# A streaming-encoder layer on one core: the first modulation's LayerNorm moves to ScalarE, and TensorE's and ScalarE's small steps between a quarter's units change order

## The chip, the cores and the metric

The kernel runs on one core of one Trainium2 chip. The metric is the device time of one execution in microseconds (us), and the number compared is the median over runs.

## The reference

One layer over 256 tokens (two blocks of 128 partitions) of width D = 2048, all in float32. What matters here is its very start:

```
ada = silu(c) @ w_ada + b_ada                  # c is one row of 2048, w_ada is 2048 x 12288
shift1, scale1, gate1, shift2, scale2, gate2 = split(ada, 6)
h = layer_norm(x) * (1 + scale1) + shift1      # x is 256 x 2048; no gain and no bias in this norm
q_a, kv_a, ... = split(h @ w_in)               # the first two slabs of 512 columns feed the attention branch
```

layer_norm subtracts the mean over the 2048 columns and multiplies by 1/sqrt(variance + 1e-5). Behind it come latent attention, a state-space branch, the merge of the two, an output projection, and an expert layer that gathers 128 rows per token from two tables. None of that is touched.

## The kernel before

Every engine runs its own hand-written list of instructions, and only semaphores tie the lists together. The first stage works in four **quarters** q = 0 to 3, each for 512 of the 2048 columns of x.

**The modulation of a quarter.** The columns of w_ada for the quarter's shift and scale (1024 columns) come in eight chunks of 1 MiB, 32 in all, numbered here c0 to c31 (c8q to c8q+7 belong to quarter q). SP issues their transfers (L585) into five buffers in turn, so chunk n waits until chunk n-5 has been used. Two 1 MiB loads of projection weights (`raw`, L572) stand behind the first chunk of quarters 1, 2 and 3, and the last two behind c31. VectorE uses the first seven chunks of a quarter (`ada1_chunks`, L1645 and L1647, two instructions a chunk, 128x1024 each), and sums into `ada1_acc`. TensorE uses the eighth, its own chunk, in `ada1_rest(q)` (L757, 32 matmuls of one column), and then adds up VectorE's partial sums over the partitions in `ada1_sums(q)` (L766, 16 matmuls of one column). `mod_quarter(q)` on VectorE (L1661, L1663) adds the bias `b_ada` and writes shift and scale to `adacol`.

**x.** Two transfers (L592) are issued behind c4. VectorE takes mean and variance (`normalise`: L1600, L1605), ScalarE the root (L1156), VectorE the reciprocal (L1595) and the normalised x in place (L1612), once for each block of tokens. TensorE transposes x in four groups (L780), ScalarE copies each out of PSUM into `xnT` (L1197).

**A quarter of h.** ScalarE applies scale and shift to the four 128-row tiles of the quarter (L1204) and rounds them to `h_hi` (L1208). VectorE takes the remainder `h_lo` (`h_quarter`, L1670). Each quarter then has two projection **units** (s = 0 and 1, one for each slab): ScalarE rounds the unit's weights to `whi` (`hi`, L1141), VectorE takes the remainder `wlo` (`lo`, L1578), and TensorE does 16 matmuls of 512 columns on `whi` (L691, L692) and 8 on `wlo` (L697) in `token_unit`. A unit starts on `h_ready` and `hi_ready`, and its last 8 matmuls wait for `lo_ready`.

**Order on each engine, as written.** VectorE: c0 to c6; the copies of `cols` and `keysT` out of PSUM (L1676, L1678), which wait for the small parameters; LayerNorm of x; then for q = 1 to 3: three chunks of quarter q, mod_quarter(q-1), one chunk, h_quarter(q-1), a chunk, lo, a chunk, lo, a chunk; at the end mod_quarter(3), h_quarter(3) and two lo. TensorE: transposes of the parameters (L741, L744, behind all 17 small loads, `params_in`); ada1_rest(0), ada1_sums(0); the transposes of x; then for each quarter both units, and behind them ada1_rest(q+1) and ada1_sums(q+1). ScalarE: SiLU of c, exp of `A_log` (which waits for `params_in`), the two roots of x, four copies of transposed x, then for each quarter scale and shift, `h_hi`, and the two `hi`.

The next stage begins with ScalarE's sums of squares of the two slabs (L1217) and a root (L1156), VectorE's `rms`, and two narrower units (L716, L717, L722).

Of the kernel before, what the change touches and what calls it, by code (L numbers as in the profile page):

```python
# [13 lines left out]
ALU = mybir.AluOpType  # L14
# [4 lines left out]
P = 128  # L19
D = 2048  # L20
# [50 lines left out]
U_LOW = 0  # L71
# [63 lines left out]
def build(nc, a, out, stop="all"):  # L135
    ctx = ExitStack()
    with ctx:
# [14 lines left out]
        def sem(name):  # L152
            return ctx.enter_context(nc.semaphore(name))
# [39 lines left out]
        x_in = at("x_in", 126 * KB, [P, BLK, D])  # L193
        xnT = at("xnT", 142 * KB, [P, DC, SEQ])
# [328 lines left out]
        ln2_step = sem("ln2_step")  # L523
        x1_ready = sem("x1_ready")
        var_ready = sem("var_ready")
        std_ready = sem("std_ready")
# [141 lines left out]
        def _(pe):  # L668
# [70 lines left out]
            pe.wait_ge(params_in, 16 * 17)  # L739
            for j, (first, n) in enumerate(((0, COLS_T1), (COLS_T1, P), (COLS_T2, COLS_ALL - COLS_T2))):  # L740
                last = nc.tensor.transpose(aux[:, 0, first:first + n], rows[0:n, j, :], ident[0:n, 0:n])  # L741
            last.then_inc(rows_turned, 1)
            for j in range(2):
                last = nc.tensor.transpose(aux[:, 1, j * P:j * P + P], krows[:, j, :], ident)  # L744
            last.then_inc(rows_turned, 1)
# [26 lines left out]
            ada1_sums(0)  # L772
            pe.wait_ge(x_normed, BLK)
            pe.wait_ge(cols_ready, 2)
# [15 lines left out]
            if on("low"):  # L790
# [10 lines left out]
                for q in range(QUARTERS):  # L801
                    pe.wait_ge(h_ready, q + 1)
                    for s in range(2):
                        token_unit(U_LOW, 2 * q + s, 0, 0, h_hi, h_lo, 4 * q, DC - 1,
                                   [ps[:, s, b, :] for b in range(BLK)], early=True)
                    if q + 1 < QUARTERS:
                        ada1_rest(q + 1)
                        ada1_sums(q + 1)
# [324 lines left out]
        def _(act):  # L1133
# [55 lines left out]
            F(csil[:, :], aux[:, 2, 0:DC], ACT.Silu).then_inc(c_ready, 1)  # L1189
            act.wait_ge(params_in, 16 * 17)  # L1190
            F(anegA[:, :], anegA[:, :], ACT.Exp).then_inc(neg_a, 1)
            for b in range(BLK):
                norm_root(b + 1)
# [6 lines left out]
            for q in range(QUARTERS):  # L1200
                act.wait_ge(h_full, q + 1)
# [7 lines left out]
                for s in range(2):  # L1209
                    hi(U_LOW, 2 * q + s, 0, 0)  # L1210
# [207 lines left out]
            if on("h2"):  # L1418
                for b in range(BLK):
                    norm_root(b + 3, b)  # L1420
                for b in range(BLK):
# [3 lines left out]
                    act.wait_ge(ln2_step, 3 * b + 1)  # L1425
                    F(minus_mean, total, ACT.Copy, scale=-1.0 / D).then_inc(ln2_step, 1)
                    act.wait_ge(ln2_step, 3 * b + 2)
                    F(ln2_junk[:, :], x1[:, b, :], ACT.Square, bias=minus_mean, accum_out=square).then_inc(ln2_step, 1)
                    act.wait_ge(ln2_step, 3 * b + 3)
# [139 lines left out]
        def _(dve):  # L1569
# [103 lines left out]
            dve.wait_ge(c_ready, 1)  # L1673
            ada1_chunks(0, 0, ADA_V)
            dve.wait_ge(rows_turned, 1)
            V.tensor_copy(cols[:, :], aux[:, 0, 0:COLS_ALL]).then_inc(cols_ready, 1)  # L1676
            dve.wait_ge(rows_turned, 2)
            V.tensor_copy(keysT[:, :, :].rearrange("p a b -> p (a b)"), aux[:, 1, 0:2 * KEYS]).then_inc(cols_ready, 1)  # L1678
            dve.wait_ge(x_loaded, 16 * BLK)
            for b in range(BLK):  # L1680
                normalise(x_in[:, b, :], x_in[:, b, :], b + 1).then_inc(x_normed, 1)
            for q in range(1, QUARTERS):
                ada1_chunks(q, 0, 3)
                mod_quarter(q - 1)
                ada1_chunks(q, 3, 4)
                h_quarter(q - 1)
                for s in range(2):
                    ada1_chunks(q, 4 + s, 5 + s)
                    lo(U_LOW, 2 * (q - 1) + s, 0, 0)
                ada1_chunks(q, 6, ADA_V)  # L1690
# [563 lines left out]
        def _(pool):  # L2254
# [87 lines left out]
            if on("all"):  # L2342
# [22 lines left out]
                for r in range(BLK * SEL):  # L2365
# [6 lines left out]
                    elif r < EARLY:  # L2372

                        pool.wait_ge(x1_stored, 16 * BLK)
                        pool.wait_ge(ln2_step, 3 * BLK)
# [74 lines left out]
```

## Time and profile before

| | us |
|---|---|
| three runs: median | 2737.41 |
| lowest and highest | 2735.43 and 2744.17 |
| span of the profiled execution, first to last instruction | 2736.6 |
| TensorE busy in it | 2371.4 (87%) |
| VectorE busy in it | 2055.5 (75%) |
| ScalarE busy in it | 1007.8 (37%) |
| GpSimd busy in it | 883.5 (32%) |

The profiled execution has no time of its own beside the span, so the span is what it is held to: it is 0.8 us under the median of the three runs. The stage that is changed is the first of many; it ends at about 148 us of the span, when the eighth projection unit is done. The rest of the span is the same code in both kernels.

### The profile page before, as it was taken

The page shows a single profiled execution, that of the slowest core. Times are in us where ns is not written, and L with a number is a line of the kernel's source. Part 1 is how long each engine was busy: PE and PEld are TensorE (multiplying, and loading weights), DVE is VectorE, ACT ScalarE, POOL GpSimd, SP SyncE. Part 2 cuts the span into 40 slices and gives each one's busy share as a digit, 9 for nine tenths or more (in the row PEclk, how much of TensorE's full clock was granted, in tenths as well). Part 3 has the DMA queues.
Part 4 walks back from the last instruction along what each step waited for, and adds up shares of the span by engine and source line. Part 5 has one row for each costly group of instructions (what it writes and reads, how often), then busy time and mean ns, then how long its engine had stood idle before and what let it go on. Part 6 is the DMA issues. An engine that isn't in the chain of part 4 may idle for free.

```text
span 2736.6 us, 38178 instructions
## 1 busy us (share of the span) xinstructions
PE 2371.4 (87%) x14404; PEld 1975.2 (72%) x14404; DVE 2055.5 (75%) x2511; ACT 1007.8 (37%) x1436; POOL 883.5 (32%) x745
## 2 busy tenths in 40 slices
PE   3799999999999999999969776666667699999994
PEld 3689999888888889999859766656566664444441
DVE  6777679778888786444575899999999786665577
ACT  2245443344444444433343222227777750000000
POOL 0000011222222220000001466656666554444354
PEclk9799999999999999999989888887777799999997
DMA  9766669566666665555745999999999879999997
GB/s 381 290 216 239 218 236 345 209 216 216 216 215 216 213 212 177 185 185 184 264 181 191 355 410 419 420 403 392 405 407 399 348 259 414 413 414 414 414 412 254
DMA packets 143723, 817.88 MB, mean 299 GB/s; under 512 B 16552, under 2 KB 19232, under 8 KB 69328
## 3 DMA queue, kind: packets, MB, share of 16 engines
q0 software_dynamic: 93200, 477.21, 44.7%
q1 hardware_dynamic: 48480, 335.95, 33.2%
q10 hardware_dynamic: 1888, 2.59, 0.3%
q8 instruction: 106, 1.74, 0.3%
q14 instruction: 49, 0.40, 0.0%
HBM read 811.46 MB, written 4.23 MB: 298 GB/s over the span
## 4 chain that ended last, share of the span: by engine, by line
PE 63%; DVE 25%; issue 4%; DMA 4%; ACT 3%; POOL 1%; ACTq 0%; DVEq 0%; POOLq 0%
PE aux L1122 15%; DVE rrow L2145 12%; PE ps L716 9%; PE ps L717 9%; PE ps L722 9%; PE ps L691 4%; PE ps L692 4%; PE ps L697 3%; DVE rrow_first L2145 2%; DVE ada_acc L1647 1%; PE aux L973 1%; DMA dskip<-in_D_skip 1%; DMA ada_in<-in_p_ada 1%; DMA vden<-in_p_vd 1%; PE aux L930 1%
## 5 line engine op out<-in xcount | busy, mean ns | idle before, releaser
L1578 DVE TENSOR_TENSOR wlo<-raw,whi 128x2048 fp32r<-128x2048 f32 x216 | 497.3, 2303 | 323.0 <-ACT whi L1141 312.8
L1141 ACT ACTIVATE whi<-raw 128x2048 fp32r<-128x2048 f32 x216 | 412.2, 1911 | 685.3 <-PE ps L722 528.0
L2175 DVE SCALAR_TENSOR_TENSOR ps<-vrow,acc,ps 128x1024 f32<-128x1024 f32 x235 | 302.6, 1288 | 176.4 <-DMA vrow<-in_p_vg,acc 156.7
L2354 POOL DMA_INDIRECT rrow<-in_peer_u,acc x222 | 359.8, 1621 | 220.1 <-DVE dots L2145 115.3
L2145 DVE CUSTOM_DVE_ANT_0 rrow<-rrow,h 128x2048 f32<-128x2048 f32 x175 | 391.1, 2289 | 9.1 <-DMA rrow<-in_peer_u,acc 8.6
L716 PE MATMUL ps<-h_hi,whi 128*128 128x256 f32 x1552 | 389.2, 291 | 1.3 <-DVE h_lo L2033 1.3
L717 PE MATMUL ps<-h_lo,whi 128*128 128x256 f32 x1552 | 377.0, 283 | 0.0
L2354 POOL DMA_INDIRECT vrow<-in_p_vg,acc x256 | 252.3, 986 | 255.5 <-DVE ps L2175 173.5
L716 PEld LDWEIGHTS ps<-h_hi,whi 128*128 128x128 f32 x1552 | 297.9, 192 | 16.2 <-issue 14.1
L717 PEld LDWEIGHTS ps<-h_lo,whi 128*128 128x128 f32 x1552 | 298.2, 192 | 5.8 <-issue 5.7
L1064 PE MATMUL aux<-hT,rT 128*128 128x128 f32 x1792 | 235.8, 295 | 72.6 <-ACT rT L1472 71.8
L1064 PEld LDWEIGHTS aux<-hT,rT 128*128 128x128 f32 x1792 | 228.1, 210 | 82.6 <-issue 68.4
L2268 POOL DMA_DIRECT2D ada_in<-in_p_ada x128 | 69.3, 542 | 675.6 <-DVEq L1734 534.3
L1122 PE MATMUL aux<-vden,wt 128*128 128x512 f32 x512 | 241.5, 594 | 0.0
L1627 DVE SCALAR_TENSOR_TENSOR acc<-ada_in,csil,acc 128x512 f32<-128x512 f32 x240 | 184.8, 770 | 37.0 <-DMA ada_in<-in_p_ada 24.2
L722 PE MATMUL ps<-h_hi,wlo 128*128 128x256 f32 x1552 | 202.1, 283 | 0.0
L722 PEld LDWEIGHTS ps<-h_hi,wlo 128*128 128x128 f32 x1552 | 193.3, 192 | 0.0
L1156 ACT ACTIVATE st<-st,con 128x2 f32<-128x2 f32 (+1 forms) x18 | 5.2, 294 | 507.4 <-DVE st L1605 507.1
L1122 PEld LDWEIGHTS aux<-vden,wt 128*128 128x128 f32 x512 | 97.8, 191 | 123.6 <-issue 123.6
L1472 ACT ACTIVATE rT<-ps 128x1024 f32<-128x1024 f32 x112 | 110.8, 1021 | 173.1 <-PE ps L1054 165.7
L1086 PE MATMUL aux<-oh 128*128 128x128 f32 x512 | 87.8, 333 | 93.8 <-ACT oh L1518 87.7
L1054 PE MATMUL ps<-con,rrow 128*128 128x128 f32 x752 | 128.5, 344 | 40.9 <-DMA rrow<-in_peer_u,acc 40.9
(353 smaller groups left out, 4318.9 us busy)
## 6 DMA issues: line engine op xcount, KB each, us to landing
raw<-in_p_in SPq DMA_DIRECT2D x104, 1024.0 KB, 4.9
ada_in<-in_p_ada POOLq DMA_DIRECT2D x128, 512.0 KB
vden<-in_p_vd SPq DMA_DIRECT2D x64, 1024.0 KB
ada_in<-in_p_ada SPq DMA_DIRECT2D x32, 1024.0 KB, 9.2
raw<-in_p_so SPq DMA_DIRECT2D x32, 1024.0 KB, 4.8
raw<-in_p_mo SPq DMA_DIRECT2D x16, 1024.0 KB, 7.1
raw<-in_p_bc SPq DMA_DIRECT2D x16, 1024.0 KB, 7.1
raw<-in_p_mix SPq DMA_DIRECT2D x16, 1024.0 KB, 4.8
```

The lines of the kernel that those rows point to most:

```text
L716: mm(o, wh, x_hi[:, k, :], start=(k == 0 and first), stop=False, skip_group_check=True)
L717: mm(o, wh, x_lo[:, k, :], start=False, stop=False, skip_group_check=True)
L722: last = mm(o, lo[:, kc, c:c + width], x_hi[:, k, :], start=False, stop=(k == klast), skip_group_check=True)
L1054: last = nc.tensor.transpose(ps[:, half, t // 4, (t % 4) * P:(t % 4) * P + P], row_tile(r)[:, c:c + P], ident)
L1064: last = mm(aux[:, 3, j * P:j * P + P], rT[:, kc, :], hT[b][:, kc, :], start=(kc == 0), stop=(kc == DC - 1), skip_group_check=True)
L1122: last = mm(aux[:, 2 * b + n, :], wt_column(b, 2 * u + q), vden[:, u % 4, q, n * W:n * W + W], start=(u == 0 and q == 0), stop=(u == NVU - ...
L1141: F(whi[:, n % 2, :, 0:cols_], raw[:, n % 4, :, 0:cols_], ACT.Copy).then_inc(hi_ready, 1)
L1578: V.tensor_tensor(wlo[:, n % 2, :, 0:cols_], raw[:, n % 4, :, 0:cols_], whi[:, n % 2, :, 0:cols_].bitcast(F32), ALU.subtract).then_inc(lo_ ...
L1627: last = V.scalar_tensor_tensor(acc_, tile[:, kc, :], csil[:, k:k + 1], acc_, ALU.mult, ALU.add)
L2145: last = V.tensor_tensor_reduce(row, row, h2[:, b, :], 1.0, 0.0, ALU.mult, ALU.add, dots[:, k, e:e + 1])
L2175: last = V.scalar_tensor_tensor(o, row, w, o, ALU.mult, ALU.add)
L2354: return G.indirect_dma_start(out=dst, out_offset=None, in_=table, in_offset=bass.IndirectOffsetOnAxis(ap=eid_all[:, r:r + 1], axis=0))
```

## The change

There are four edits.

1. The statistics of x move from VectorE to ScalarE: for each block a Copy that sums, the negated mean, a Square around the mean that sums, and the root (three steps on `x_step`, with the scratch tile `x_junk` at the place of `xnT`). VectorE only takes the reciprocal and the product of the negated mean with it (`mean_and_root`), and ScalarE then writes the normalised x with one Identity per block. exp of `A_log` moves behind it. Since `x_step` and the later second norm share a semaphore, the later waits are raised by 6.
2. TensorE's transposes of the parameters move from ahead of ada1_rest(0) to behind ada1_sums(0), and VectorE's copies of their results from ahead of quarter 1 into it, behind its first two chunks. mod_quarter(q-1) comes behind two chunks of quarter q instead of three, and everything behind it follows one chunk earlier.
3. ada1_rest(q+1) goes between a quarter's two units, and ada1_sums(q+1) behind the second.
4. ScalarE rounds the first weights of a quarter (`hi` of unit 2q) ahead of the wait for that quarter's shift and scale, not behind `h_hi`.

```diff
--- before.py
+++ after.py
@@ -191,6 +191,7 @@
         h2 = at("h2", 110 * KB, [P, BLK, D])
 
         x_in = at("x_in", 126 * KB, [P, BLK, D])
+        x_junk = at("x_junk", 142 * KB, [P, D])
         xnT = at("xnT", 142 * KB, [P, DC, SEQ])
         oT = at("oT", 126 * KB, [P, DC, SEQ])
         cqT_hi = at("cqT_hi", 142 * KB, [P, RC, SEQ], F32R)
@@ -521,8 +522,10 @@
         row_used = sem("row_used")
         scale_plus = sem("scale_plus")
         ln2_step = sem("ln2_step")
+        x_step, x_steps = ln2_step, 3 * BLK
         x1_ready = sem("x1_ready")
         var_ready = sem("var_ready")
+        x_scaled = var_ready
         std_ready = sem("std_ready")
         fin_ready = sem("fin_ready")
         out_done = sem("out_done")
@@ -736,13 +739,6 @@
             pe.wait_ge(con_in, 16)
             pe.wait_ge(c_in, 16)
             nc.tensor.transpose(aux[:, 2, 0:DC], crow[:, :], ident[0:DC, 0:DC]).then_inc(c_turned, 1)
-            pe.wait_ge(params_in, 16 * 17)
-            for j, (first, n) in enumerate(((0, COLS_T1), (COLS_T1, P), (COLS_T2, COLS_ALL - COLS_T2))):
-                last = nc.tensor.transpose(aux[:, 0, first:first + n], rows[0:n, j, :], ident[0:n, 0:n])
-            last.then_inc(rows_turned, 1)
-            for j in range(2):
-                last = nc.tensor.transpose(aux[:, 1, j * P:j * P + P], krows[:, j, :], ident)
-            last.then_inc(rows_turned, 1)
 
             ada_sum = aux[:, 3, :]
 
@@ -770,8 +766,14 @@
             pe.wait_ge(c_ready, 1)
             ada1_rest(0)
             ada1_sums(0)
+            pe.wait_ge(params_in, 16 * 17)
+            for j, (first, n) in enumerate(((0, COLS_T1), (COLS_T1, P), (COLS_T2, COLS_ALL - COLS_T2))):
+                last = nc.tensor.transpose(aux[:, 0, first:first + n], rows[0:n, j, :], ident[0:n, 0:n])
+            last.then_inc(rows_turned, 1)
+            for j in range(2):
+                last = nc.tensor.transpose(aux[:, 1, j * P:j * P + P], krows[:, j, :], ident)
+            last.then_inc(rows_turned, 1)
             pe.wait_ge(x_normed, BLK)
-            pe.wait_ge(cols_ready, 2)
             for r in range(4):
                 if r >= 2:
                     pe.wait_ge(xT_ready, r - 1)
@@ -803,9 +805,8 @@
                     for s in range(2):
                         token_unit(U_LOW, 2 * q + s, 0, 0, h_hi, h_lo, 4 * q, DC - 1,
                                    [ps[:, s, b, :] for b in range(BLK)], early=True)
-                    if q + 1 < QUARTERS:
-                        ada1_rest(q + 1)
-                        ada1_sums(q + 1)
+                        if q + 1 < QUARTERS:
+                            (ada1_sums if s else ada1_rest)(q + 1)
 
                 for k in range(2):
                     channel_unit(U_LOW, 8 + k, 0, 0, h_hi, h_lo, DC // 2 * k, DC - 1,
@@ -1187,10 +1188,25 @@
 
             act.wait_ge(c_turned, 1)
             F(csil[:, :], aux[:, 2, 0:DC], ACT.Silu).then_inc(c_ready, 1)
+            act.wait_ge(con_in, 16)
+            act.wait_ge(x_loaded, 16 * BLK)
+            for b in range(BLK):
+                total, minus_mean, square = (st[:, 52 + 3 * b + j:53 + 3 * b + j] for j in range(3))
+                if b:
+                    act.wait_ge(x_step, 3 * b)
+                F(x_junk[:, :], x_in[:, b, :], ACT.Copy, accum_out=total).then_inc(x_step, 1)
+                act.wait_ge(x_step, 3 * b + 1)
+                F(minus_mean, total, ACT.Copy, scale=-1.0 / D).then_inc(x_step, 1)
+                act.wait_ge(x_step, 3 * b + 2)
+                F(x_junk[:, :], x_in[:, b, :], ACT.Square, bias=minus_mean, accum_out=square).then_inc(x_step, 1)
+                act.wait_ge(x_step, 3 * b + 3)
+                root(st[:, 46 + 4 * b:47 + 4 * b], square, 1.0 / D)
+            for b in range(BLK):
+                act.wait_ge(x_scaled, b + 1)
+                F(x_in[:, b, :], x_in[:, b, :], ACT.Identity, scale=st[:, 46 + 4 * b:47 + 4 * b],
+                  bias=st[:, 44 + 4 * b:45 + 4 * b]).then_inc(x_normed, 1)
             act.wait_ge(params_in, 16 * 17)
             F(anegA[:, :], anegA[:, :], ACT.Exp).then_inc(neg_a, 1)
-            for b in range(BLK):
-                norm_root(b + 1)
 
             for r in range(4):
                 act.wait_ge(x_turned, r + 1)
@@ -1198,6 +1214,7 @@
                   psf[:, 1024 * (r % 2):1024 * (r % 2) + 1024], ACT.Copy).then_inc(xT_ready, 1)
 
             for q in range(QUARTERS):
+                hi(U_LOW, 2 * q, 0, 0)
                 act.wait_ge(h_full, q + 1)
                 act.wait_ge(xT_ready, 4 + q)
                 for k in range(4 * q, 4 * q + 4):
@@ -1206,8 +1223,7 @@
                 last.then_inc(xT_ready, 1)
                 act.wait_ge(xT_ready, 4 + q + 1)
                 F(h_hi[:, 4 * q:4 * q + 4, :], xnT[:, 4 * q:4 * q + 4, :], ACT.Copy).then_inc(h_hi_ready, 1)
-                for s in range(2):
-                    hi(U_LOW, 2 * q + s, 0, 0)
+                hi(U_LOW, 2 * q + 1, 0, 0)
             if on("low"):
                 def sumsq(s):
                     for b in range(BLK):
@@ -1422,11 +1438,11 @@
                     act.wait_ge(x1_ready, b + 1)
                     total, minus_mean, square = (st[:, 52 + 3 * b + j:53 + 3 * b + j] for j in range(3))
                     F(ln2_junk[:, :], x1[:, b, :], ACT.Copy, accum_out=total).then_inc(ln2_step, 1)
-                    act.wait_ge(ln2_step, 3 * b + 1)
+                    act.wait_ge(ln2_step, x_steps + 3 * b + 1)
                     F(minus_mean, total, ACT.Copy, scale=-1.0 / D).then_inc(ln2_step, 1)
-                    act.wait_ge(ln2_step, 3 * b + 2)
+                    act.wait_ge(ln2_step, x_steps + 3 * b + 2)
                     F(ln2_junk[:, :], x1[:, b, :], ACT.Square, bias=minus_mean, accum_out=square).then_inc(ln2_step, 1)
-                    act.wait_ge(ln2_step, 3 * b + 3)
+                    act.wait_ge(ln2_step, x_steps + 3 * b + 3)
                     root(st[:, 46 + 4 * b:47 + 4 * b], square, 1.0 / D)
                 for b in range(BLK):
                     for q in range(4):
@@ -1671,23 +1687,31 @@
                                 h_hi[:, 4 * q:4 * q + 4, :].bitcast(F32), ALU.subtract).then_inc(h_ready, 1)
 
             dve.wait_ge(c_ready, 1)
+            def mean_and_root(b):
+
+                rsqrt(st[:, 46 + 4 * b:47 + 4 * b], b + 1)
+                V.tensor_tensor(st[:, 44 + 4 * b:45 + 4 * b], st[:, 53 + 3 * b:54 + 3 * b], st[:, 46 + 4 * b:47 + 4 * b],
+                                ALU.mult).then_inc(x_scaled, 1)
+
             ada1_chunks(0, 0, ADA_V)
-            dve.wait_ge(rows_turned, 1)
-            V.tensor_copy(cols[:, :], aux[:, 0, 0:COLS_ALL]).then_inc(cols_ready, 1)
-            dve.wait_ge(rows_turned, 2)
-            V.tensor_copy(keysT[:, :, :].rearrange("p a b -> p (a b)"), aux[:, 1, 0:2 * KEYS]).then_inc(cols_ready, 1)
-            dve.wait_ge(x_loaded, 16 * BLK)
             for b in range(BLK):
-                normalise(x_in[:, b, :], x_in[:, b, :], b + 1).then_inc(x_normed, 1)
+                mean_and_root(b)
             for q in range(1, QUARTERS):
-                ada1_chunks(q, 0, 3)
+                ada1_chunks(q, 0, 2)
+                if q == 1:
+                    dve.wait_ge(rows_turned, 1)
+                    V.tensor_copy(cols[:, :], aux[:, 0, 0:COLS_ALL]).then_inc(cols_ready, 1)
+                    dve.wait_ge(rows_turned, 2)
+                    V.tensor_copy(keysT[:, :, :].rearrange("p a b -> p (a b)"), aux[:, 1, 0:2 * KEYS])\
+                        .then_inc(cols_ready, 1)
+                    dve.wait_ge(cols_ready, 1)
                 mod_quarter(q - 1)
-                ada1_chunks(q, 3, 4)
+                ada1_chunks(q, 2, 3)
                 h_quarter(q - 1)
                 for s in range(2):
-                    ada1_chunks(q, 4 + s, 5 + s)
+                    ada1_chunks(q, 3 + s, 4 + s)
                     lo(U_LOW, 2 * (q - 1) + s, 0, 0)
-                ada1_chunks(q, 6, ADA_V)
+                ada1_chunks(q, 5, ADA_V)
             mod_quarter(QUARTERS - 1)
             h_quarter(QUARTERS - 1)
             for s in range(2):
@@ -2372,7 +2396,7 @@
                     elif r < EARLY:
 
                         pool.wait_ge(x1_stored, 16 * BLK)
-                        pool.wait_ge(ln2_step, 3 * BLK)
+                        pool.wait_ge(ln2_step, x_steps + 3 * BLK)
                         pool.wait_ge(x1_ready, BLK)
                     elif r < EARLY + 4:
```

## Rows read from the trace of the kernel before

**Rows 1.** Timeline, 0 to 59 us: start, duration, engine, line, form, count, idle before it.

```profile
26.03 5.33 DVE L1647 SCALAR_TENSOR_TENSOR ada_acc<-ada_in,csil,ada_acc 128x1024 f32<-128x1024 f32 x4 [2.07 <-DMA ada_in<-in_p_ada]
...
35.20 0.86 PE L741 MATMUL aux<-con,rows 120*128 120x120 f32 x3 [30.70 <-DMA dskip<-in_D_skip]
...
36.29 6.83 PE L757 MATMUL aux<-csil,ada_in 128*128 128x1 f32 x32
...
46.05 0.74 DVE L1645 TENSOR_SCALAR ada_acc<-ada_in,csil 128x1024 f32<-128x1024 f32 x1
...
46.39 5.86 PE L780 MATMUL ps<-con,x_in 128*128 128x128 f32 x32
...
50.08 3.23 ACT L1197 ACTIVATE xnT<-ps 128x1024 f32<-128x1024 f32 x3 [0.68 <-PE ps L780]
```

**Rows 2.** Timeline, the modulation of quarter 0 and the start of quarter 1's.

```profile
53.43 0.16 DVE L1661 TENSOR_TENSOR adacol<-aux,cols 128x4 f32<-128x4 f32 x1
...
53.83 2.07 ACT L1204 ACTIVATE xnT<-xnT,adacol 128x256 f32<-128x256 f32 x4 [0.52 <-DVE adacol L1663]
...
56.90 3.70 ACT L1141 ACTIVATE whi<-raw 128x2048 fp32r<-128x2048 f32 x2
57.09 1.23 DVE L1670 TENSOR_TENSOR h_lo<-xnT,h_hi 128x1024 fp32r<-128x1024 f32 x1 [0.79 <-ACT h_hi L1208]
...
58.93 0.77 PE L691 MATMUL ps<-whi,h_hi 128*128 128x512 f32 x1 [6.68 <-ACT whi L1141]
...
78.12 0.16 DVE L1661 TENSOR_TENSOR adacol<-aux,cols 128x4 f32<-128x4 f32 x1
```

**Rows 3.** Timeline, VectorE: a chunk that was late, and quarter 3's modulation.

```profile
99.71 5.25 DVE L1647 SCALAR_TENSOR_TENSOR ada_acc<-ada_in,csil,ada_acc 128x1024 f32<-128x1024 f32 x4 [2.21 <-DMA ada_in<-in_p_ada]
...
129.26 0.16 DVE L1661 TENSOR_TENSOR adacol<-aux,cols 128x4 f32<-128x4 f32 x1 [7.18 <-PE aux L766]
```

**Rows 4.** Stretches: from:to, us, busy by engine, PEclk, DMA share, GB/s.

```profile
58.93:77.80 18.87, 18.82 (x96) 16.18 (x96) 18.30 (x14) 1.66 (x1) 0.00 (x0) 0.86 0.85 321
110.49:129.25 18.76, 18.73 (x96) 16.15 (x96) 11.41 (x8) 1.66 (x1) 0.00 (x0) 0.86 0.53 213
58.93:67.06 8.13, 8.13 (x25) 6.51 (x26) 7.99 (x6) 1.66 (x1) 0.00 (x0) 0.68 1.01 419
118.50:123.93 5.43, 5.43 (x27) 4.49 (x26) 3.54 (x3) 0.00 (x0) 0.00 (x0) 1.00 0.36 124
123.93:129.25 5.32, 5.29 (x47) 5.21 (x47) 0.00 (x0) 0.00 (x0) 0.00 (x0) 0.98 0.00 0
129.25:134.76 5.51, 0.00 (x1) 0.04 (x1) 1.66 (x4) 5.08 (x7) 0.00 (x0) 0.50 0.00 0
158.40:166.00 7.60, 7.60 (x51) 7.60 (x52) 7.22 (x23) 1.86 (x3) 0.00 (x0) 0.78 0.75 277
```

**Rows 5.** Tile ln_junk: the same two steps in the later norm, durations in ns min/median/max.

```profile
L1424 ACT ACTIVATE ln_junk<-x x2: 1909/1909/1909, 1410.2 to 1415.0; 128x2048 f32<-128x2048 f32 x2
...
L1428 ACT ACTIVATE ln_junk<-x,st x2: 2002/2002/2002, 1412.5 to 1417.3; 128x2048 f32<-128x2048 f32 x2
```

**Rows 6.** Stretches of ten us: transfers at full load, and with a pause.

```profile
20.00:30.00 10.00, 0.00 (x0) 0.00 (x0) 7.67 (x6) 0.00 (x0) 0.00 (x0) 1.00 1.00 395
...
70.00:80.00 10.00, 7.75 (x60) 7.24 (x58) 9.50 (x11) 1.49 (x3) 0.00 (x0) 0.89 0.72 257
```

**Rows 7.** Timeline, SP: the issue of c20, c21 and c22.

```profile
76.00 1.29 SPq L585 DMA_DIRECT2D ada_in<-in_p_ada  x3
```

**Rows 8.** Timeline, TensorE behind the changed stage: two short stops.

```profile
156.41 0.41 PE L817 MATMUL aux<-con,dk 128*128 128x128 f32 x2 [0.90 <-ACT dk L1242]
158.37 0.39 PE L716 MATMUL ps<-cqT_hi,whi 128*128 128x256 f32 x1 [1.55 <-DVE wlo L1578]
```

**Rows 9.** Timeline, ScalarE: a table load behind the changed stage, and what follows it.

```profile
150.75 1.28 ACT L1238 ACT_TABLE_LOAD   x1
152.05 0.40 ACT L1238 ACTIVATE sin<-angs 128x64 f32<-128x64 f32 x2
```

## The prediction

> **What bounds the kernel now.** I read first the timeline of the first 60 us, then that of VectorE and TensorE to the end of the changed stage, then stretches for the clock and the transfers. About 0.8 us lies between the profiled span and the median, so differences of the span are taken over as they are. What measurement can tell from no change is 0.3%, about 8.2 us.
>
> The start [rows 1]: c5 arrives at 26.0, VectorE is done with c6 at 31.4 and then waits for TensorE's transposes of the parameters, which start at 35.20 when the last small load is in. Copies and LayerNorm of x follow, and quarter 1's first chunk is used only at 46.05. TensorE meanwhile works through its own chunk and the sums (36.29 to 46.39, 10.1 us), transposes x in 5.86 us, and ScalarE ends its last copy at 53.3. The modulation of quarter 0 is at 53.43 [rows 2], so there VectorE's list and the path of x end together. That is the place to look at twice: freeing one of the two gives only the distance to the other.
>
> From then on one pattern repeats [rows 2]. From mod_quarter to the end of h_lo are 4.89 us (53.43 to 58.32), and TensorE starts the quarter at 58.93, 5.50 us behind mod_quarter, because the first `whi` (half of a pair of 3.70 us from 56.90) is ready at 58.8, half a us behind h_lo. From the end of h_lo to the next mod_quarter are 19.80 us (58.32 to 78.12) of VectorE without a pause: six chunks of at most 2.65 [rows 1] and two `lo`. TensorE's share of a quarter, two units, its own chunk and the sums, is 18.87 and 18.76 us [rows 4]. VectorE leads in the first two quarters. In quarter 2 it also waited 2.21 us for c25, which came in at 99.6; quarter 3's modulation at 129.26 waited 7.18 us for TensorE's sums [rows 3]. So the last quarter is TensorE's, and it starts at 129.26 + 5.50 = 134.76. Everything later hangs on that start.
>
> **The change part by part.**
>
> *Statistics on ScalarE.* The two passes are known from the later norm, 1.91 and 2.00 us [rows 5]. x stands just ahead of c5 in the queue, one MiB takes 2.65 us at 395 GB/s [rows 6], so x is in by 23.4. With 1 us a block allowed for the small steps and one table load of 1.28 [rows 9], ScalarE has the second root at 23.4 + 2 x 4.9 + 1.3 = 34.5; VectorE adds 0.4, and the two Identity passes, priced as the Copy of 1.91, end at 38.9. Moving exp of `A_log` behind them costs nothing: its result is used much later.
>
> *TensorE's start.* Its own chunk c7 is in two transfers behind c5, at 31.3 [rows 1, 6]. Own chunk and sums 10.1, up to 41.4; transposes of the parameters 1.1 (35.20 to 36.29), up to 42.5. The normalised x has been there since 38.9 (cover 3.6 us; if ScalarE needs more than that, every us counts). Transposes 5.86, up to 48.4, last copy 1.1, 49.5. ScalarE now does `hi` of unit 0 ahead of the scaling, 1.9, so that scaling starts at 51.4 in place of 53.83. mod_quarter(0) isn't late: VectorE uses c8 and c9, copies the parameters, and passes it near 45. Then it uses c10 (to 48) and stands still for some 7 us until h_hi. This is where the 14.7 us that VectorE saves (31.4 to 46.05) go: all but 2.4 become waiting. h_lo ends at 58.32 - 2.4 = 55.9, and with `whi` ready the quarter's units start 0.13 behind it, at 56.05 in place of 58.93.
>
> *The chunk order.* Behind h_lo come four chunks instead of three, and ahead of the next mod_quarter two instead of three: again six chunks and two `lo`, 19.80. VectorE would pass mod_quarter(1) at 75.7.
>
> *Weights ahead.* TensorE starts 4.89 + 0.13 = 5.0 behind mod_quarter in place of 5.50: 0.5 us, which count where the quarter's path runs through it. `hi` has its data: the last pair of loads stands behind c31, and from 110.49 to 129.25 the transfers were busy for only 0.53 of the time [rows 4], so they were done before 121. Were one late, the scaling behind it on ScalarE would be late by as much.
>
> *Transfers.* c12 waits for TensorE's use of c7, now done near 38 instead of 43. c20 waited for TensorE's use of c15 and was issued at 76.00 [rows 7], and the transfer engines idled 0.28 of the ten us around it, 2.8 us [rows 6]. With c15 used between the units (56.05 + 8.13 + 3.5 = 67.7) that wait goes. Against it, c16 is issued when c11 is used, and that is now behind h_lo (58.5 instead of 56.3), 2.1 later. I take the difference: c25 comes at 98.9, within bounds of 96.8 and 99.6. VectorE wants it at 97.8, so mod_quarter(2) is no earlier than 98.9 + 2.6 = 101.5.
>
> *Own chunk between the units.* In sum TensorE's 18.8 us stay the same. Its sums are then done at 56.05 + 18.87 = 74.9, ahead of VectorE. But 32 matmuls of one column, 3.5 us (two thirds of the 5.32 us that they and the 16 of the sums take), now stand between two units of 512 columns. In the rows [rows 4] the granted clock was at the higher level (2.4 GHz) in a second unit (1.00, 5.43 us), and after 5.3 us of one-column work it had fallen to the lower (1.2 GHz): 0.98 up to 129.25, 0.50 in the pause behind. A shorter slack shows too: behind the stage TensorE stopped 0.9 us, did two small transposes, and stopped 1.55 us more [rows 8], and in the stretch that followed the clock was 0.78, so 0.44 of 7.6 us at the lower level, 3.3 us, of which half, 1.7, is lost [rows 4]. The new gap lies between the two in length. Call the loss in a quarter p: below 0, as no such dip; the row nearest in length gives 1.7, which I take for each of three quarters; at the most every matmul of the own chunk and of the second unit runs at half rate, 3.5 + 5.4 = 8.9.
>
> The Trainium skill (TensorE: Matmul & The Clock Gate, HAM oscillation) says that a pause between bursts of matmuls throttles the clock again, so that each burst starts at the lower rate; it speaks against this edit. By it each second unit starts slow, as a first one does (8.13 against 5.43), so p would be 2.7 and the sum below put the last start at 135.6 instead of 132.6; that the clock falls behind long one-column work, the rows agree.
>
> *A table load.* exp now stands behind the roots, so the root for the first slab must load its table again, 1.28 us [rows 9]. It falls while unit 7 runs (5.4 us), most of it covered; bounds 0 and 1.3, taken 0.3. The Trainium skill (ScalarE: Activation LUTs, What ACT_TABLE_LOAD costs) puts 2.66 us on a switch, a drain with it; the row shows the next activation 1.30 behind the load's start, and the row decides.
>
> **The sum, p = 1.7.** Sums of quarter 1: 56.05 + 18.87 + 1.7 = 76.6 (VectorE 75.7), start of its units 81.6. Sums of quarter 2: 81.6 + 18.8 + 1.7 = 102.1 (c25 allows 101.5), start 107.1. Sums of quarter 3: 107.1 + 18.8 + 1.7 = 127.6, against 129.26. Start of the last units 132.6, against 134.76: 2.2 us. With the table load 1.9, so 2737.4 - 1.9 = 2735.5.
>
> **The rivals.**
>
> *No dip* (p = 0). Modulations at 75.7, 101.5 (c25 leads), 101.5 + 5.0 + 18.8 = 125.3, last start 130.3: 4.5 earlier, 2733.2 with the table load. For it: the gap is shorter than the 5.3 us behind which the fall shows. Against: the dip behind the two short stops.
>
> *A full second warm-up*, p of 2.4 to 3. The last start is 127.5 + 3p, so at 2.4 the gain is gone; at 3, 136.5: 1.7 later, 2739.4. No change that can be measured.
>
> *Slower.* One mechanism: the clock goes down during each own chunk and stays down through the second unit. With p = 8.9 the last start is 127.5 + 26.7 = 154.2, 19.4 later: 2757. It becomes measurable from p = 5.1 on. Against: a first unit after a pause of 5.5 us got through in 8.13 at a mean of 0.68, so the clock came back within it.
>
> *VectorE's saving goes through.* If the path of x is shorter than worked out (TensorE at full rate at the start), VectorE leads, and the floor is the transfers: what they idled, some 4 us up to c25 and about as much behind it, gives at most 8 us: 2729.4. Against: TensorE's one-column matmuls took 6.83 us there.
>
> *It doesn't act.* If x is normalised later than 46.4, the start doesn't move, and with the dips the time is 2738 to 2740.
>
> **How the numbers follow.** Forecast with dips 0.42, no dip 0.28, full warm-up 0.14, no action 0.05, VectorE's saving 0.07, slower 0.04. The first four are all within 0.3% (0.89). Faster by more takes the far end of the fifth and errors of several terms: 0.07. Slower: 0.04. The range takes in all but the fifth's end and the slower case: 2730 to 2741; the forecast's own is 2733 to 2738, by c25's bounds, the table's and p of 1 to 2.4.
>
> **What the profile would show.** Units of quarter 0 start near 56, behind a stand of VectorE of some 7 us between c10 and h_lo; ScalarE's roots near 34.5; own chunk of quarter 1 at 64 to 68, c20 issued near 71; a clock below 1.00 in the second units; modulation of quarter 3 near 127.6; a new table load at L1156 near 140. Wrong would make it above all a start far from 56 (the rate of the first one-column matmuls), and p.

## The result, and the profile after

The changed kernel takes 2745.26 us (median of 9 executions, 2742.28 to 2749.39) against 2736.54 for the kernel before (9, 2733.95 to 2744.17). The ratio is 1.0029, with a 95% interval of 1.0021 to 1.0038: a slowdown of 0.3%, some 8 us, where 1.9 us of gain were forecast. The profiled execution took 2742.28 us, its fastest, and its span is 2740.6, so 1.7 us lie between the two.

The stage that was changed did what was forecast of it. Timeline of the changed kernel, 20 to 56 us, all engines:

```profile
31.40 6.96 PE L753 MATMUL aux<-csil,ada_in 128*128 128x1 f32 x32 [27.09 <-DMA ada_in<-in_p_ada]
...
33.36 0.29 ACT L1157 ACTIVATE st<-st,con 128x1 f32<-128x1 f32 x1
33.56 4.06 ACT L1206 ACTIVATE x_in<-x_in,st 128x2048 f32<-128x2048 f32 x2
...
38.22 3.55 PE L762 MATMUL aux<-con,ada_acc 128*128 128x1 f32 x16
...
42.69 4.17 PE L782 MATMUL ps<-con,x_in 128*128 128x128 f32 x24
...
50.95 2.06 ACT L1221 ACTIVATE xnT<-xnT,adacol 128x256 f32<-128x256 f32 x4
...
54.20 1.23 DVE L1686 TENSOR_TENSOR h_lo<-xnT,h_hi 128x1024 fp32r<-128x1024 f32 x1 [6.64 <-ACT h_hi L1225]
...
55.48 0.79 PE L694 MATMUL ps<-whi,h_hi 128*128 128x512 f32 x1 [7.29 <-DVE h_lo L1686]
```

Read it against [rows 1, 2]. TensorE's first work moves from 35.20 to 31.40, the second root is at 33.36, the normalised x is there at 37.6 (33.56 + 4.06) and waits for TensorE, and VectorE stands still for 6.64 us ahead of `h_lo`: what it saved became waiting. The quarter's units start at 55.48 instead of 58.93. The steps of VectorE and the last quarter's first unit, timelines of the same kernel:

```profile
75.66 0.16 DVE L1677 TENSOR_TENSOR adacol<-aux,cols 128x4 f32<-128x4 f32 x1
...
98.27 2.60 DVE L1663 SCALAR_TENSOR_TENSOR ada_acc<-ada_in,csil,ada_acc 128x1024 f32<-128x1024 f32 x2 [0.59 <-DMA ada_in<-in_p_ada]
...
101.55 0.16 DVE L1677 TENSOR_TENSOR adacol<-aux,cols 128x4 f32<-128x4 f32 x1 [0.68 <-PE aux L762]
...
126.39 0.16 DVE L1677 TENSOR_TENSOR adacol<-aux,cols 128x4 f32<-128x4 f32 x1 [5.11 <-PE aux L762]
...
131.26 0.79 PE L694 MATMUL ps<-whi,h_hi 128*128 128x512 f32 x1 [4.91 <-DVE h_lo L1686]
```

From quarter 2 on each modulation waits for TensorE's sums (101.55 and 126.39), and the last units start 3.5 us earlier than before (131.26 against 134.76 in the prediction's sum). Stretches of the changed kernel show what the new place of the own chunk costs (columns as in [rows 4]): an own chunk between the units, the three second units, and quarter 2's whole share.

```profile
62.78:66.53 3.75, 3.75 (x33) 3.75 (x32) 3.68 (x4) 1.34 (x1) 0.00 (x0) 0.93 1.01 428
66.53:73.42 6.89, 6.89 (x25) 5.59 (x26) 6.10 (x6) 0.57 (x1) 0.00 (x0) 0.79 0.98 369
...
92.40:99.61 7.21, 7.21 (x27) 5.72 (x27) 6.26 (x7) 1.91 (x1) 0.00 (x0) 0.76 1.02 425
...
117.56:124.51 6.95, 6.95 (x25) 5.64 (x26) 3.65 (x3) 0.00 (x0) 0.00 (x0) 0.78 0.23 85
...
106.49:126.35 19.86, 19.86 (x96) 17.06 (x96) 14.54 (x10) 2.33 (x2) 0.00 (x0) 0.82 0.63 257
```

The second unit of each quarter ran at a mean granted clock of 0.76 to 0.79 instead of 1.00. With the own chunk ahead of it, it took 10.6 us (3.75 + 6.89; then 3.49 + 7.21 and 3.67 + 6.95) instead of 8.9 (3.5 of the 5.32 us of one-column work in [rows 4], and 5.43): 1.7, 1.8 and 1.7 us.

A quarter's whole share grew by other amounts: 19.78, 20.85 and 19.86 us, against 18.87, 18.78 and 18.76 in the kernel before, so 0.9, 2.1 and 1.1. The first units make most of the difference: they took 7.30, 8.31 and 7.40 us, where the kernel before has 8.13, 7.78 and 8.01.

**Where the loss comes in.** ScalarE's sums of squares of the second slab close the stage. Timeline of ScalarE, the changed kernel:

```profile
139.82 1.28 ACT L1157 ACT_TABLE_LOAD   x1
...
143.84 0.60 ACT L1233 ACTIVATE junk<-ps 128x512 f32<-128x512 f32 x1 [1.47 <-PE ps L700]
```

and the same sum of squares in the kernel before:

```profile
148.05 0.60 ACT L1217 ACTIVATE junk<-ps 128x512 f32<-128x512 f32 x1 [2.75 <-PE ps L697]
```

That is 4.2 us ahead. The new table load isn't free on the way: it holds up the root and the weights behind it, and TensorE waits for `wlo`, which it did not in the kernel before. Timeline of TensorE, the changed kernel:

```profile
144.31 0.39 PE L719 MATMUL ps<-h_hi,whi 128*128 128x256 f32 x1 [0.52 <-DVE wlo L1601]
```

By 156 us TensorE is 4.2 us ahead again, so this wait is made good. Matching instructions further down, the changed kernel stays ahead, by 5.1 us at 771. Then comes VectorE's loop of the state-space stage (`with dve.Fori(1, 4)`, L1959 before and L1983 after), whose three rounds have the same code in both. VectorE across its two jumps back, the changed kernel:

```profile
771.08 1.01 DVE L1977 TENSOR_SCALAR yg<-yg,st 128x512 f32<-128x512 f32 x2
779.04 0.49 DVE L1641 TENSOR_SCALAR acc<-ada_in,csil 128x512 f32<-128x512 f32 x1 [6.95 <-issue]
...
915.21 1.01 DVE L1977 TENSOR_SCALAR yg<-yg,st 128x512 f32<-128x512 f32 x2
922.86 0.49 DVE L1641 TENSOR_SCALAR acc<-ada_in,csil 128x512 f32<-128x512 f32 x1 [6.64 <-issue]
```

and the kernel before:

```profile
776.22 1.01 DVE L1953 TENSOR_SCALAR yg<-yg,st 128x512 f32<-128x512 f32 x2
777.39 0.49 DVE L1625 TENSOR_SCALAR acc<-ada_in,csil 128x512 f32<-128x512 f32 x1 [0.16 <-issue]
...
913.41 1.01 DVE L1953 TENSOR_SCALAR yg<-yg,st 128x512 f32<-128x512 f32 x2
914.56 0.48 DVE L1625 TENSOR_SCALAR acc<-ada_in,csil 128x512 f32<-128x512 f32 x1
```

The shift (after minus before) goes from -5.1 to +1.7 over the first jump and from +1.8 to +8.3 over the second, and stays near +7 on TensorE until 1570. "issue" in the brackets means that VectorE waited for nothing that the profile shows. The queue of the instructions shows it. The transfers of the changed kernel in 774 to 781 us (queue, kind: packets, MB, share), the row of q14, the queue that reads VectorE's instructions (e3 below shows whose it is):

```profile
q14 instruction: 3, 0.02, 1.2%
```

Three reads of 8 KiB, at 774.7, 777.2 and 779.6, about 2.4 us apart; two lie in the stop, and the third begins 0.5 us after it. Between 745 and 1060 us there are ten in the changed kernel, five behind each jump, and none in the kernel before. The page of the changed kernel, its span and section 3, has

```profile
span 2740.6 us, 38182 instructions
...
q14 instruction: 59, 0.48, 0.0%
```

where the page before has

```profile
q14 instruction: 49, 0.40, 0.0%
```

So the loop's code was read again behind each jump. The loop itself is unchanged; what is new is that VectorE's list is 9 instructions shorter ahead of it (3902 in the trace against 3911, since most of LayerNorm is gone), so that the loop stands elsewhere relative to the 8 KiB pieces in which the list is read. I take a piece to hold 128 instructions, 64 bytes each; e3 bears that out.

The Trainium skill (Runtime: NRT & Kernel Launch, Instruction fetch mechanics) says that an engine has a small instruction memory, refilled in sequence by a DMA queue of its own, and that a taken jump to a target outside what it holds forces a read before execution goes on. The trace agrees with the forced read. The page's block is 16 KiB, the reads of q14 here are of 8 KiB, and the measurement decides; the other instruction queue on the page of the profile, q8, did read 16 KiB at a time (106 reads, 1.74 MB).

### The profile page after: what moved, and what is told of

Read it like the earlier page. It is cut to its first block, busy times and chain, and to the rows that moved or that the text cites. A ratio compares the mean times of both kernels' runs of the same rounds, so it can differ in the third digit from the quotient of the medians.

```text
span 2740.6 us, 38182 instructions
## 1 busy us (share of the span) xinstructions
PE 2377.4 (87%) x14404; PEld 1973.7 (72%) x14404; DVE 2050.0 (75%) x2501; ACT 1021.8 (37%) x1449; POOL 884.6 (32%) x745
## 3 DMA queue, kind: packets, MB, share of 16 engines
q8 instruction: 106, 1.74, 0.2%
## 4 chain that ended last, share of the span: by engine, by line
PE 49%; DVE 23%; DMA 14%; issue 6%; ACT 5%; POOL 2%; ACTq 0%; DVEq 0%; POOLq 0%
DMA vrow<-in_p_vg,acc 12%; DVE rrow L2169 10%; PE ps L719 9%; PE ps L720 9%; PE ps L725 9%; PE ps L694 4%; PE ps L695 4%; PE ps L700 4%; DVE rrow_first L2169 2%; DVE ps L2199 2%; POOL vrow L2378 1%; PE aux L974 1%; DMA rrow<-in_peer_u,acc 1%; PE aux L1087 1%; PE aux L931 1%
## 5 line engine op out<-in xcount | busy, mean ns | idle before, releaser
L2199 DVE SCALAR_TENSOR_TENSOR ps<-vrow,acc,ps 128x1024 f32<-128x1024 f32 x235 | 302.7, 1288 | 175.5 <-DMA vrow<-in_p_vg,acc 145.7
```

Of the source, the lines that this page charges most:

```text
L2199: last = V.scalar_tensor_tensor(o, row, w, o, ALU.mult, ALU.add)
```

## The experiments

The theory: the first stage gains about 4 us, and the place of VectorE's loop costs the rest. The rivals: the loss comes from the first stage's dips, or from the later stages' transfers being met at other times. All kernels but e2 and e8 are built on the changed kernel.

**e1: the nine instructions back.** Nine increments are added ahead of the loop by splitting two that were there (`ROWS` is 8).

```diff
-            dve.sem_inc(ada2_used, 4)
+            for n in (2, 1, 1):
+                dve.sem_inc(ada2_used, n)
...
-            dve.sem_inc(row_used, ROWS)
+            for _ in range(ROWS):
+                dve.sem_inc(row_used, 1)
```

> The changed kernel with VectorE's list made nine instructions longer at its head (two semaphore increments split into several of smaller size, while VectorE waits for the first data), so that its loop in the state-space stage stands as far into the list as in the kernel before. Theory (instruction fetch): in the changed kernel VectorE stopped 6.95 us and some 6 us at the two jumps back of that loop, with three reads of 8 KiB each on the instruction queue, because the loop stands nine instructions further forward. Then the stops and the reads are gone, the last units of the first stage still start near 131.3, and the time is that of before less some 4 us: 2732, ratio 0.9985. Rival (the later stages suffer from the shift in time itself, or from scatter): the stops stay, 2742 to 2749.

Measured: 2731.88 us (11 executions) against 2736.18, ratio 0.9991 (0.9979 to 1.0002). Nothing else differs from the changed kernel, and it is 13 us faster by the medians, some 10 by the two ratios. Against the kernel before, the interval takes in 1, so a gain of the four edits is likely but not clear of noise. Waits of VectorE, first in the changed kernel, then in e1 (what waited <- for what: us in total, times, longest):

```profile
DVE acc L1641 <- issue: 13.8, 3, 6.9
```

```profile
DVE acc L1643 <- issue: 0.2, 1, 0.2
```

and e1's page again has

```profile
span 2728.6 us, 38191 instructions
...
q14 instruction: 49, 0.40, 0.0%
```

The two stops are gone and with them the 13 us, while the first stage, dips included, is within 0.9 us of the changed kernel's (modulations at 76.01, 102.19 and 127.22, last units at 132.09). That the dips cause the loss is out.

**e2, e3: the same shift by other means.** If only the place counts, 119 instructions more (128 less 9) must put the kernel before into the same state, and 128 more must leave the changed kernel in it. The additions are waits that are already fulfilled, which take half an instruction each here: 238 ahead of the loop in the kernel before (e2), 256 in the changed kernel (e3).

```diff
             dve.sem_inc(row_used, ROWS)
+            for _ in range(238):
+                dve.wait_ge(lo_ready, 4)
```

> The kernel before with 119 more instructions at the head of VectorE's list (waits that are already fulfilled, two to an instruction), no other edit. 119 is 128 less 9, so if the list is fetched in pieces of 128 instructions (8 KiB), the loop stands in its pieces as in the changed kernel. Theory (instruction fetch): two stops of 6 to 7 us at the jumps back of the state-space loop, which the kernel before doesn't have: about 2736.5 + 13 = 2749, or somewhat less where slack takes some. Rival (scatter or the edits themselves): 2736 to 2739, no stops.

> The changed kernel with 128 more instructions at the head of VectorE's list (fulfilled waits). Control for e1: the list is longer, but by one whole piece of 128. Theory (instruction fetch, pieces of 128): the stops stay and the time is that of the changed kernel, 2745. Rival (any lengthening helps): 2732.

Measured: e2 2750.21 us (4 executions), ratio 1.0057 (1.0041 to 1.0072); e3 2747.09 (4), 1.0041 (1.0026 to 1.0057). VectorE's wait at the loop's head in e2, then in e3:

```profile
DVE acc L1627 <- issue: 14.1, 3, 7.0
```

```profile
DVE acc L1643 <- issue: 14.2, 3, 7.1
```

e2 has none of the four edits. Against the kernel before, its shift is -0.2 us at 725, +6.5 at 846 and +13.4 at 966: two stops of 6.9 and 7.0 that TensorE takes on whole. A kernel without the change thus shows the slowdown, and the changed kernel keeps it at a distance of one whole piece. In e3 the whole execution has 60 reads of q14, one more than the changed kernel's 59: 128 instructions more in VectorE's list alone are one read of 8 KiB more, so q14 is VectorE's, and 64 bytes an instruction fit. e2 has 60 too, against 49 in the kernel before: ten at the loop and one for its 119.

The added waits have a price of their own at the head: VectorE uses its first chunk at 13.50 us in e2 (11.32 before) and at 14.38 in e3 (11.22 in the changed kernel). In e2 nothing of it is left at the last units (134.22). In e3 they start at 134.79, 3.5 later than in the changed kernel, and that can make the 2 us by which e3 is slower.

**e9, e7: between.** 80 and 180 such waits in the changed kernel, 40 and 90 instructions, so 31 and 81 behind the place of the kernel before.

> The changed kernel with 40 more instructions at the head of VectorE's list, to see whether e1 works because of the number nine (the place of before) or because of a whole range of places. Theory (pieces of 128; the loop's 325 instructions touch three pieces only if it begins within the first 50 or so of one): it begins some 31 to 40 into a piece, no read on the instruction queue between the loop's first round and its end, no stops, 2732 as e1. Rival (only the place of before is free of stops): stops as in e7, 2741 or more.

> The changed kernel with 90 more instructions at the head of VectorE's list. Theory (instruction fetch, pieces of 128, and a place for few pieces; the loop has 325 instructions by the trace, so it touches three pieces only if it begins within the first 50 or so of one): the loop begins some 81 to 90 into a piece, touches four, and the two stops are there, 2745. Rival (any lengthening between 9 and 128 removes them): no stops, 2732.

Measured: e9 2732.63 us (8), ratio 0.9987 (0.9973 to 1.0001), no stop and no read of q14 between 745 and 1060 us. e7 2741.62 (8), ratio 1.0022 (1.0012 to 1.0032): slower, as the theory had it, but by less than the changed kernel and than the 2745 expected. VectorE at e7's first jump:

```profile
773.64 1.01 DVE L1979 TENSOR_SCALAR yg<-yg,st 128x512 f32<-128x512 f32 x2
779.22 0.49 DVE L1643 TENSOR_SCALAR acc<-ada_in,csil 128x512 f32<-128x512 f32 x1 [4.57 <-issue]
```

Five reads behind each jump again, but the stop is one read of 2.4 us shorter (reads at 777.2 and 779.6, so one lies in it and not two). Its whole wait there is 8.9 us against 13.8. So there are three states of the same loop: no read (places 0 and +31), stops of 4.6 and 4.3 (+81), stops of 7 (-9, which is +119). Both expectations came true in kind by some luck. They counted the 325 instructions that the trace has of a round, which would touch three or four pieces, and the reads are of five. So the loop is longer than what the trace has of it, or some reads run ahead of need.

**e4: the own chunk back behind both units.** e1 with edit 3 undone.

```diff
-                        if q + 1 < QUARTERS:
-                            (ada1_sums if s else ada1_rest)(q + 1)
+                    if q + 1 < QUARTERS:
+                        ada1_rest(q + 1)
+                        ada1_sums(q + 1)
```

> e1 with the third edit undone: TensorE's own chunk and the sums stand behind both units of a quarter again. By the terms of the prediction (p, the dip of the granted clock behind the gap): no dip in the second units, modulation of quarter 1 at 75.7 by VectorE, of quarter 2 near 100.9 by the transfers, of quarter 3 near 124.6, last units start near 129.5 in place of 131.26, so 1.8 us faster than e1. Rival (the own chunk between the units is worth something, since its buffer is free earlier): the transfers come later, and the last units start at 131 or later.

Measured: 2729.38 us (11), ratio 0.9976 (0.9967 to 0.9985), 2.5 under e1 by the medians. The profile is of its slowest execution (2736.93), and contradicts the simple picture that this place is free. Its stretches, quarter 1's share, then own chunk and sums in it alone:

```profile
80.95:102.90 21.95, 21.86 (x96) 19.11 (x96) 19.15 (x14) 2.34 (x2) 0.00 (x0) 0.73 1.01 413
...
94.66:102.82 8.16, 8.16 (x49) 8.07 (x47) 5.69 (x5) 1.06 (x1) 0.00 (x0) 0.64 1.01 410
```

Here the clock fell within the own chunk itself, in two of three quarters, the one-column work took 8.16 us and then 7.96 instead of the 5.32 of [rows 4], and the last units started at 134.61 after all. In the kernel before the clock fell only within the sums (1.93, 2.20 and 1.97 us instead of 1.84).

The profiles of all runs together say what each place costs. With the own chunk behind both units (the kernel before, e2, e4, e5, e6) TensorE's share of a quarter is 18.7 to 18.9 us in twelve of fifteen, and 21.8 to 22.0 in the three where the clock fell within the own chunk (two in e4, one in e6). With it between them (the changed kernel, e1, e3, e7, e8, e9) all eighteen take 19.8 to 21.2. The second unit is 6.89 to 7.21 us in fourteen of these, and 8.25 to 8.35 in four (one each in e1, e7, e8 and e9), each behind an own chunk of 3.9 to 4.0 us instead of 3.5. So the old place is cheaper in most quarters and dearer in some; the median puts it ahead, and the intervals of e1 and e4 meet.

**e8: edit 3 alone in the kernel before.**

> The kernel before with the third edit alone: TensorE's own chunk between a quarter's two units, the sums behind the second. VectorE's list keeps its length, so no stops at the state-space loop. Terms of the prediction: c25 comes earlier, so VectorE's wait of 2.2 us for it goes or shrinks, which brings mod_quarter(2) to about 103; a dip of the granted clock in each second unit costs 1.7 us, so quarter 3's modulation is near 128.8 to 129.5 in place of 129.26: 2736 to 2737, no change. Rival (no dip): 127.1, 2734.5. Rival (full second warm-up, 3 us a quarter): 2738 to 2739.

Measured: 2738.38 us (10), ratio 1.0005 (0.9996 to 1.0014): no change, and the number is the rival's. The dip is there without the other edits. e8's second units of quarters 0 and 2:

```profile
69.17:76.20 7.03, 7.03 (x25) 5.71 (x26) 6.63 (x7) 0.00 (x0) 0.00 (x0) 0.77 0.89 352
...
121.11:129.46 8.35, 8.35 (x25) 6.62 (x26) 0.56 (x1) 0.00 (x0) 0.00 (x0) 0.65 0.10 41
```

The second of them is as slow as a first unit after a pause (8.13). The modulation of quarter 3 is at 131.34, not at 128.8 to 129.5, and the last units start at 136.84, 2.1 later than before. e8 has the loop in its old place, and no stop.

**e5: the first weights back behind `h_hi`.** e4 with edit 4 undone.

```diff
-                hi(U_LOW, 2 * q, 0, 0)
                 act.wait_ge(h_full, q + 1)
...
-                hi(U_LOW, 2 * q + 1, 0, 0)
+                for s in range(2):
+                    hi(U_LOW, 2 * q + s, 0, 0)
```

> e4 (own chunk behind both units, VectorE's list nine longer) with the fourth edit undone too: the first weights of a quarter are rounded behind h_hi again. Theory (the prediction's term): TensorE starts a quarter 5.5 us behind mod_quarter in place of 4.9, so the last units start 0.6 us later, and more where TensorE leads, up to 0.6 in each quarter; ScalarE's scaling of quarter 0 starts 1.9 us earlier, since hi isn't ahead of it, so quarter 0's units start only some 0 to 0.6 us later. Together 2730 against 2729.4. Rival (rounding ahead is worth more than the prediction says): 2732 or more.

Measured: 2732.54 us (12), ratio 0.9986 (0.9974 to 0.9998), 3.2 over e4 by the medians, with intervals that meet; the number is the rival's (2732 or more), but its executions lie between 2727.63 and 2740.74. Its profiled execution (2728.08) shows both sides. The scaling of quarter 0 starts at 49.45, not 50.95, since no `whi` stands ahead of it where x is late, and the units start at 54.56; in the later quarters TensorE waits for `whi` and starts 5.50 us behind the modulation (73.75 to 79.25) instead of 4.94 (75.66 to 80.60). What the edit is worth in sum is not settled by it: e5's profile is near its fastest execution, e4's is of its slowest.

**e6: x transposed ahead of the sums.** If VectorE's 6.64 us of standstill are TensorE's order, putting the transposes of x right behind the own chunk of quarter 0, ahead of its sums and of the parameters' transposes, should turn them into time. e4 and

```diff
             ada1_rest(0)
-            ada1_sums(0)
-            pe.wait_ge(params_in, 16 * 17)
...
             pe.wait_ge(x_normed, BLK)
...
+            ada1_sums(0)
+            pe.wait_ge(params_in, 16 * 17)
```

> e4 with one more edit: TensorE transposes x straight behind its own chunk of quarter 0, and the sums and the transposes of the parameters come behind x. Theory (after the change the path of x through TensorE bounds the start, and VectorE stands still for it): x is transposed at 38.4 to 43.6 in place of 42.7 to 48.2, mod_quarter(0) comes near 48, h_lo of quarter 0 ends near 53 in place of 55.4 to 56.2, VectorE's stop ahead of it shrinks by as much, and the last units start up to 2.5 us earlier than in e4: 2727. Rival (the start isn't what bounds, the transfers are): h_lo is earlier and the wait for c25 grows by as much: 2729, as e4.

Measured: 2725.95 us (5), ratio 0.9962 (0.9949 to 0.9975): the fastest of all, 3.4 under e4 by the medians, though the two intervals still meet. TensorE and VectorE in e6:

```profile
38.30 6.17 PE L774 MATMUL ps<-con,x_in 128*128 128x128 f32 x32
44.30 1.84 PE L762 MATMUL aux<-con,ada_acc 128*128 128x1 f32 x16
...
52.33 0.79 PE L694 MATMUL ps<-whi,h_hi 128*128 128x512 f32 x1 [5.59 <-DVE h_lo L1689]
```

```profile
47.40 0.15 DVE L1680 TENSOR_TENSOR adacol<-aux,cols 128x4 f32<-128x4 f32 x1
...
51.05 1.22 DVE L1689 TENSOR_TENSOR h_lo<-xnT,h_hi 128x1024 fp32r<-128x1024 f32 x1 [0.79 <-ACT h_hi L1226]
```

The standstill shrinks to 0.79 us, from 6.64 in the changed kernel and 6.04 in e4, and the units start at 52.33, not 56.26 as in e4. The sums also run in 1.84 us here, not 3.55: the granted clock rose at 43.4, during the transposes (128 columns each) ahead of them.

## Why the prediction was wrong

**The step that failed** is the first paragraph's "differences of the span are taken over as they are", with "everything later hangs on that start". The sum ended at the start of the last units and carried its 1.9 us over the remaining 2600 us because the code there is the same. The code is, but its place in VectorE's list is not. e1 and e2 show that the place alone makes 13 to 14 us by the medians: 2731.88 with the loop where it was, 2745.26 with it 9 instructions earlier; 2736.18 and 2750.21 without the change. None of the rivals had it; the slower one (2757, through the clock) was another mechanism, and e1 refutes it. Section 3 of the page and the diff were enough to raise it: the reads of q14, a loop, and a list that becomes shorter ahead of it. They gave no price.

**The first stage, term by term** (forecast, then the changed kernel's profile):

- Second root 34.5, measured 33.36; normalised x 38.9, measured 37.6; standstill of VectorE 7, measured 6.64. Right.
- Start of quarter 0's units 56.05, measured 55.48. `hi` ahead of the scaling put it at 50.95 (forecast 51.4).
- Modulations 76.6, 102.1 and 127.6, measured 75.66, 101.55 and 126.39; in the first VectorE led, at its own 75.7, since TensorE's share took 19.78 us and not 18.87 + 1.7 = 20.57. c25 at 98.9, measured 98.27, and, as forecast, TensorE and not the transfer led there.
- The dip p of 1.7 from the two short stops of [rows 8] and [rows 4]: 1.7, 1.8 and 1.7 measured on the own chunk and the second unit. But the sum adds p to a quarter's whole share, and there it was 0.9, 2.1 and 1.1, since the first units changed too; that the size fits is in part luck. A second unit at full rate (no dip) is in none of the six profiles with this order. One as slow as in a full warm-up is not in the changed kernel's, but once in each of four others.
- `whi` ahead: 5.0 behind the modulation, measured 4.94 (75.66 to 80.60).
- Table load at 140, taken as 0.3: it stands at 139.82 and made TensorE wait 0.52 us for `wlo`, which was made good by 156 us.
- Last units 132.6, measured 131.26: a gain of 3.5 where 2.2 was forecast; the start was 0.57 earlier and the three shares 1.1 shorter in sum than forecast. With the loop in its place (e1) the medians give 4.3 less than before, the ratio 0.9991 some 2.5, with an interval that takes in 1; the forecast had 1.9.

So the mechanism and nearly every size, p apart, held in the stage that was read, and the sign of the whole was decided in one that wasn't.

**Open.** In the last stage VectorE waited 13.7 us in 7 waits for issue (`ps`, L2199) in the changed kernel, 1.9 in one before, 3.7 in two in e1 and 5.6 in three in e2. The code there is also placed elsewhere, but e2 is slower by 14 us with little of these waits, so they aren't needed for the loss. No run separates them. In the changed kernel's profile 3 of the 7 us were made good again by the end (span 2740.6 against 2736.6); which wait absorbs them is not shown. No run separates the first edit from the second, so the 3.5 us of the first stage are not shared out between them. Why the four places give none, one or two reads in the stop was not tried in finer steps: five distinct pieces read in each round would fit a memory that holds four and a loop that touches a fifth, but that is argued only.

## What to carry to other kernels

An edit that adds or removes instructions ahead of a loop can move the loop across a boundary of the pieces in which code is read: look at the engine's instruction queue in section 3 and for waits on "issue" at the loop's head in both kernels before the difference is put down to the edit, and try the same edit with its length restored. When one of two lists that end together is freed, ask which order on the other gives the saved time back: e6 moved a few lines on TensorE and took 5.2 us of standstill out of VectorE (6.04 in e4, 0.79 in e6). One-column matmuls between units of 512 columns cost the following unit 1.5 to 2.9 us of clock here (6.89 to 8.35 against 5.43), so they are not free filler.

## What the runs showed of the hardware

- VectorE's code was read in pieces of 8 KiB, the first two or three behind a jump about 2.4 us apart. A jump back of this loop stopped the engine for 6.6 to 7.1 us (changed kernel, e2, e3), 4.3 and 4.6 us (e7), or 0.2 (all others), for the same loop, by its place modulo 128 instructions.
- A fulfilled wait isn't free: 238 of them were placed as 119 instructions and moved the loop like 119, and VectorE's first use of data came 2.2 us later (e2; 256 of them, 3.2 us in e3).
- With e4's order the granted clock went down to 1.2 GHz during one-column matmuls of an own chunk (4.75 us instead of 3.63) in some quarters and not in others; e6, with the same order, shows it once (4.58). In the kernel before the clock fell only behind the own chunks, within the sums (1.93 to 2.20 us instead of 1.84).
- A table load on ScalarE, 1.28 us, was followed by the next activation 1.30 us behind its start (139.82 to 141.12 in the changed kernel).
